# A chunked recurrence with its middle rounds written out three times, or once inside a hardware loop

## The reference, cut to what matters

```python
def wkv7_step(state, inp):
    r, w, k, v, a, b = inp
    sa = jnp.einsum('...ij,...j->...i', state, a)
    state = (state * w[..., None, :] + sa[..., :, None] * b[..., None, :]
             + v[..., :, None] * k[..., None, :])
    y = jnp.einsum('...ij,...j->...i', state, r)
    return state, y
...
    _, y = lax.scan(wkv7_step, init, xs)
    y = jnp.moveaxis(y, 0, 2)
    y_sum = y[0] + jnp.flip(y[1], axis=1)
```

## Time and profile before

| | before |
|---|---|
| median of 3 runs | 4714.32 us (4712.31 to 4718.0) |
| the profiled execution, its own time | 4712.31 us |
| its span, first to last instruction | 4710.5 us |
| PE busy | 4378.9 us, 93% |
| DVE / ACT / POOL busy | 53% / 34% / 7% |
| mean granted TensorE clock | 0.961 |

### The profile page before, as it was taken

One profiled execution on the slowest core, in us unless ns is written; L12 is line 12 of the kernel. 1 busy time (PEld: TensorE's weight loads), 2 busy tenths in 40 slices (PEclk: granted clock), 3 DMA queues, 4 the chain that ended last, 5 costly groups with the idle time before them and its releaser, 6 DMA issues. The chain is left out here.

```text
span 4710.5 us, 76455 instructions
## 1 busy us (share of the span) xinstructions
PE 4378.9 (93%) x31788; PEld 3321.7 (71%) x31788; DVE 2497.3 (53%) x4059; ACT 1609.4 (34%) x2467; POOL 320.8 (7%) x307
## 2 busy tenths in 40 slices
PE   8898999899999989999998899978998999999987
PEld 7675788676688767888887744446877666776775
DVE  3634543433445341777777369953544346566663
ACT  2324322322322131666665210133222223433432
POOL 0120000000000000111111000000000012222220
PEclk9899999998999999999999999989998999999998
DMA  3201222221122232211111221111221310000101
GB/s 147 108 19 72 90 90 107 76 89 72 54 104 93 94 125 94 64 52 59 55 56 43 107 90 72 72 54 72 101 104 59 138 37 20 20 20 20 55 4 54
DMA packets 36630, 337.04 MB, mean 72 GB/s; under 512 B 4080, under 2 KB 6384, under 8 KB 18544
## 3 DMA queue, kind: packets, MB, share of 16 engines
q1 hardware_dynamic: 36336, 332.76, 19.3%
HBM read 320.16 MB, written 12.58 MB: 71 GB/s over the span
## 5 line engine op out<-in xcount | busy, mean ns | idle before, releaser
L539 PE MATMUL ps<-hi,weight_parts 128*128 128x512 f32 x5136 | 1609.1, 394 | 122.3 <-DVE lo L406 76.8
L539 PEld LDWEIGHTS ps<-hi,weight_parts 128*128 128x128 f32 x5136 | 978.7, 191 | 341.8 <-issue 123.6
L539 PE MATMUL ps<-lo,weight_parts 128*128 128x512 f32 x2568 | 1010.7, 394 | 0.0
L527 DVE TENSOR_TENSOR weight_parts<-w,weight_parts 128x1024 fp32r<-128x1024 f32 (+1 forms) x336 | 407.0, 1213 | 968.5 <-ACT weight_parts L518 968.2
L518 ACT ACTIVATE weight_parts<-w 128x1024 fp32r<-128x1024 f32 (+1 forms) x336 | 351.7, 1048 | 1200.8 <-PE ps L539 996.5
L539 PEld LDWEIGHTS ps<-lo,weight_parts 128*128 128x128 f32 x2568 | 489.8, 191 | 102.0
L3527 PEld LDWEIGHTS ps<-buffers 64*64 64x64 f32 x12544 | 419.1, 136 | 115.0 <-issue 112.9
L3527 PE MATMUL ps<-buffers 64*64 64x64 f32 x12544 | 444.9, 226 | 45.0 <-issue 17.6
L2409 PE MATMUL ps<-x_parts,column_parts 128*128 128x512 f32 x1536 | 360.7, 392 | 10.5 <-DVE column_parts L2643 9.9
L2884 PE MATMUL ps<-x,w 128*128 128x512 f32 x768 | 331.6, 595 | 6.8 <-PEq L815 6.8
L2409 PEld LDWEIGHTS ps<-x_parts,column_parts 128*128 128x128 f32 x1536 | 286.6, 189 | 69.9 <-DVE column_parts L2643 10.3
(11 more groups left out here) (481 smaller groups left out, 5334.4 us busy)
## 6 DMA issues: line engine op xcount, KB each, us to landing
w<-in_weights SPq DMA_DIRECT2D x126, 2048.0 KB, 7.9
w<-in_wh SPq DMA_DIRECT2D x64, 512.0 KB, 4.0
v_kept<-buffers SPq DMA_DIRECT2D x4, 1024.0 KB, 5.2
buffers<-v_kept SPq DMA_DIRECT2D x16, 256.0 KB, 2.6
h<-x_kept SPq DMA_DIRECT2D x2, 2048.0 KB, 10.5
x<-in_xT SPq DMA_DIRECT2D x4, 512.0 KB, 11.3
x_kept<-h SPq DMA_DIRECT2D x1, 2048.0 KB, 7.2
vc_kept<-x SPq DMA_DIRECT2D x4, 512.0 KB, 2.6
```

Of the source, the lines that this page charges most:

```text
L527: dve.tensor_tensor(K.parts[:, j % 2, 1, 0:nk, :], part_of(K, slot, j, nk, by_row), K.parts[:, j % 2, 0, 0:nk, :].bitcast(F32), ALU.subtra ...
L539: mm = pe.matmul(ps, K.parts[:, j % 2, m, k, :], x[:, k * T:(k + 1) * T], start=(first and k == 0 and n == 0), stop=(last and k == nk - 1 ...
```

## The change

The loop over `r` in `rounds` becomes a hardware loop on each engine that calls it (GpSimd, TensorE, ScalarE and VectorE). The body, four steps, stands in the instruction stream once and is executed three times. `r` is now a register's value, and with it `n`, `c` and all that follows from them. Buffer parities (`par`, `o`) stay constants.

```diff
         step(0, 0, 0, 0, None, None, 0)
         step(1, 1, 0, 0, 0, 0, 0)
-        for r in range(3):
+        with eng.Fori(0, 3) as r:
             for o in range(2):
                 c = 2 * r + 1 + o
                 par = (1 + o) % 2
```

## The result

The changed kernel takes 4752.59 us (median of 4 runs, 4749.88 to 4754.67), the one before 4713.32 us beside it (4 runs, 4712.29 to 4718.0). The ratio is 1.0081, with an interval of 1.0063 to 1.0099: 39 us, or 0.8%, slower. I had forecast 4727, with a range that ended at 4743. The direction was right; the size was nearly three times what I had said.

A forecast was written before the change was run, and what follows sets the result against it. TensorE, at the edge of its instruction supply, was taken to bound the kernel; branches 8.0, register instructions 4.7 and waits 0.7 summed to 13.4 us over the profiled 4712.3, giving a forecast of 4727 us, range 4710 to 4743.

The forecast's parts named there:

- The branches: Two taken branches on TensorE, each with a bare fetch of 4.0 us because the body has left instruction memory: 8.0 us.
- The other engines' branches: VectorE, ScalarE and GpSimd branch at the same step boundary, covered by TensorE's 16 projection matmuls: costed at nothing.
- The register instructions: On TensorE, 77 a step fill packets; paid where fetch is the limit, 2.6 packets a step at 0.15 us: 4.7 us.
- the upper bound: Most that TensorE's register instructions could cost, if all 90 packets of the stretch paid: 13.5 us.
- Idle time without a releaser: Sign on TensorE: idle time that ends with no semaphore should grow from 13.5 to about 26 us.
- Waits of VectorE and ScalarE: A register instruction carries the wait ahead of VectorE's copy, 0.02 us on each of 35 chain waits: 0.7 us.
- Layout: Packet ends repeat each round; the stretch could be 5.0 us shorter or 5.2 longer for that alone; taken as 0.
- at the same microsecond: Sign on TensorE: the idle pieces inside the three rounds should repeat at the same places.
- It costs nothing: Rival: body's top still in memory or fetched in time, register instructions hidden; 4715 us, chance 0.24.
- faster: Rival: the one repeated layout happens to be good, gaining 18.5 us against 8.4 for branches; 4704 us, chance 0.08.
- The sequencer's lead is lost: Rival: register instructions between two waits show on TensorE, 9 us, plus late packets and full fetches; 4747 us, chance 0.10.

## Why the forecast was too low

| part, us in the stretch | forecast | measured | from |
|---|---|---|---|
| two branches, idle | 8.0 | 7.3 | waits of L3594 |
| low clock after them | none | about 4.4 | clock record, windows |
| register instructions alone | 4.7 | 22.8 | the run without a loop |
| waits for the chain | 0.7 | 0.3 | 15.9 - 15.6 |
| both branches, net | 8.0 | 6.5 to 7.4 | differences to the run without a loop |
| whole stretch | 13.4 | 30.2 | windows |

*The branches: right.* The body of 31 packets does not stay in TensorE's instruction memory, the fetch lies bare, and it takes 3.5 us in place of the 4.0 that I took. A loop of 5 packets costs 0.2 us a round, one of 31 costs 3.5 us; where between them the limit lies, no run here shows. The Trainium skill, page "Runtime: NRT & Kernel Launch", section "Instruction fetch mechanics", says that a branch to a target outside the window has to wait for a DMA fetch; the trace agrees, and adds the price. The section has two sizes for that window, TensorE's memory of 2,048 instructions, by which I went, and two pages of 256. The trace does not agree with two pages: the loop of about 1,200 instructions, 5 packets, fetched nothing in five rounds.

*The other engines' branches: right.* They cost nothing, shown by the run in which only they loop, and for VectorE the reason given holds too: it fetches, its next instruction comes 2.8 us after the branch, and TensorE's projection matmuls cover that. Its body is 590 instructions a round (1,769 in the stretch). ScalarE, with 310, goes on after 0.2 us, so there was nothing to cover.

*The clock: missed.* A bare fetch is an idle piece of 3.6 us, and the granted clock fell to 1.2 GHz behind it, for 6.8 us. That is about 2.2 us each time. In the net difference it doesn't show as an addition: fetch and clock together would be 11.7 us, and the difference to the run without a loop is 6.5 to 7.4. Two waits are shorter in the looped kernel than in that run. The idle time at L3527 without a releaser is 2.5 us less (27.3 against 29.8), perhaps since a packet that comes with the branch is one that is not late elsewhere. And that run has one wait for ScalarE that neither kernel has:

```profile
PE ps L3527 <- ACT buffers L3775: 1.5, 1, 1.5
```

With TensorE's busy time (579.4 against 575.3) that closes the sum: 7.3 + 4.1 - 2.5 - 1.5 = 7.4.

*The register instructions: the step that failed.* The prediction has: "Where the fetch is the limit, that is paid. The pieces of idle time number 19 / 12 = 1.6 a step, and I add one packet a step that is at the limit now and goes over it: 2.6 x 0.15 x 12 = 4.7 us." The mechanism was the right one, and the size was off by a factor of nearly five. Even the upper bound, all 90 packets at 0.15 us, gives 13.5 and was passed. Two things were wrong in it. The number of places: the idle pieces went from 19 to 39, 1.7 more a step in place of one. And the price of one: I had counted only the array's work that a packet loses. But the spacing of packets in the earlier trace rows holds an idle part of 1.2 to 1.5 us already, and once a packet that was just in time is late, its whole idle piece is new: (27.3 - 13.5) / 20 = 0.7 us for each new piece, and not 0.15.

A cleaner way to put it is a price for each instruction that TensorE's sequencer takes in these steps, and five runs give it:

| sequencer instructions in the stretch | stretch, us | us for one, against before |
|---|---|---|
| about 240 (semaphores taken out) | 576.5 | 0.054 |
| 672 (before) | 599.9 | |
| about 1,100 (half as many added) | 619.8 | 0.046 |
| about 1,540 (added at each wait) | 637.6 | 0.043 |
| 749 more, registers (without a loop) | 622.7 | 0.030 |
| 440 more, register moves | 617.5 | 0.040 |

The four rows of semaphore instructions lie nearly on a straight line through the kernel before, so they show no threshold that the added instructions cross: the straight code was limited already by what its queue can deliver in the dense pieces, and each instruction there has its price in time. The register rows lie below that line. I had read this limit off and then applied it to 2.6 packets a step. The number of register instructions, too, was 64 a step (766 / 12) and not 77. Idle time without a releaser was to grow from 13.5 to about 26 us; with the two pieces at L3594 it is 34.6.

*TensorE's busy time: missed.* It grew by 9.2 us, with the same matmuls. Some 4.4 are the low clock. For the other 4.8 I have an inference only: the record of a 64x64 matmul is 218 ns long while a pair of them follows the last every 58 ns or so, so at each stop the ends of the last matmuls, about 0.16 us, are counted as busy; 20 more stops make 3.2 us. In the run without a loop, where the clock was full, busy time grew by 5.1, with 17 more stops that would make 2.7. With the semaphore instructions taken out it fell by 7.0, with 18 fewer stops that would make 2.9. So this is a part of it at most, and the rest is open.

*Waits of VectorE and ScalarE: small, as forecast.* They measured 0.3 us in place of 0.7, which is too little to say more.

*Layout: open.* I took 0. The three rounds of the changed kernel have 7.4, 9.2 and 10.7 us of such idle time at L3527, so even one layout, run three times, does not give one result. The pieces lie in the same four regions of each round (37 to 50, 83 to 102, 139 to 155 and 185 to 206 us from its start), not at the same microsecond as I had said they would.

*From the stretch to the 39 us.* Between the profiled executions lie 33.6 us: 30.2 in the stretch and 4.1 in the part after it, less 1.6 in the start, and 0.9 outside the span from first to last instruction. The other 5.7 are that the profiled execution of the changed kernel lies 6.7 us below its median and that of before 1.0. Why the part after the stretch grew by 4.1 us wasn't tried. It doesn't take a loop: in the run with register moves the same part, with the same code, took 217.4 us, and in the run without a loop 211.8.

*The rivals.* "It costs nothing" falls with the 3.5 us branches, "faster" with it. "The sequencer's lead is lost" gave 4747, nearest to the result, with packets at the limit as one of its terms. But its own mechanism, a register instruction between two waits ahead of an empty array, would show in the waits for the chain, and these grew by 0.3 us in all.

Still open are three points: whether places in a packet or the sequencer's time is what is paid, as said; whether a hint close to the branch would do anything; and how the loop does with the semaphore instructions taken out. The last wasn't tried. By the runs here it would have to beat 4681 us with two bare fetches and 64 register instructions a step more, and nothing speaks for that. The fastest kernel measured here is the one written out, without the increments.

## What to carry to other kernels

Where small matmuls follow each other densely, count the instructions between them: waits, increments and register work that look hidden behind the array cost 0.03 to 0.05 us each here, where its idle time ends with no releaser and a new instruction packet. The cheapest gain here was to take such instructions out, before anything is moved or reordered. A hardware loop on the engine that sets the end pays twice, with a bare fetch at each taken branch if its body is large (3.5 us, and the clock behind it), and with a register instruction for each count that depends on the round; on engines that wait anyway the same loop was free, even with 2.8 us of bare fetch on VectorE. The record of a branch does not show such a fetch on every engine; the start of the next instruction does.

## What the runs showed of the hardware that I had not expected

- One more semaphore instruction costs 0.043 to 0.054 us of wall time between 64x64 matmuls and nothing between those of 512 columns (384 more of them: ratio 0.9993, 0.9984 to 1.0002). The Trainium skill, in the section named above, says that the fetch of instructions is hidden, since the sequencer issues more slowly than its memory is filled. The traces here do not agree for dense stretches: stops of up to 1.6 us end with a packet, already in the kernel before.
- A taken branch on TensorE takes 208 ns if its target is still in memory and 3.4 to 3.6 us if not, and announcing it at the top of the round changed nothing. On VectorE the record of a taken branch is 63 ns, but its next instruction starts 2.8 us later with a body of 590 instructions; on ScalarE, with 310, it starts 0.2 us later.
- The granted clock fell to 1.2 GHz in each of the six idle pieces ahead of L3594 in the three kernels with a loop on TensorE (3.5 to 3.7 us long), five times for 6.8 us and once for 3.4. In the run without a loop, with idle pieces of up to 1.5 us, it stayed at 1.00 for the whole stretch. With 45 pieces of up to 1.8 us, in the run with a semaphore instruction more at each wait, it fell once, for 3.4 us; with 34 and 32 pieces of up to 1.8 us, in the runs with half as many and with register moves, it never fell.
